# Index queries in packed chunks of 512, the index key beside two heads' queries, and three chunks in turn: one decoder layer on one core

## What is computed

```
h = rms_norm(x, norm_gain)                            # 256 x 2048
proj = einsum('bsd,dn->bsn', h, w_in)
qa, ka, va, ga   1024 columns each   # branch A: 8 heads x 128, sparse attention, its gate
qi 1024, ki 64, wi 16                # the index: 16 heads x 64, one shared key, 16 weights
qb, kb, vb, gb   1024 columns each   # branch B: differential attention, its gate
ma, mb           2048 columns each   # merge gates
qa, ka, qb, kb = rope(rms_norm(head, gain))           # per head of 128
qi, ki = rope(qi), rope(ki)                           # per head of 64, no norm
score = sum_h relu(qi_h . ki) * wi_h ; the top 64 keys of each query are kept in branch A
x + (sigmoid(ma) * (oa*silu(ga)) @ w_o_a + sigmoid(mb) * (ob*silu(gb)) @ w_o_b) @ w_out
```

## Time and profile before

| | us |
|---|---|
| median of 3 runs | 776.13 (774.92 to 776.16) |
| the profiled execution | 776.79 |
| its span | 775.0 |
| TensorE matmuls busy | 770.0 of 775.0 |
| VectorE busy | 510.5 |
| ScalarE busy | 423.6 |
| GpSimd busy | 132.8 |
| granted TensorE clock | 1.00 |

### The profile page before, as it was taken

How to read it: one execution, slowest core, us unless ns; L and a number is a source line. 1 busy time by engine, 2 the same in 40 slices (tenths; PEclk the granted TensorE clock), 3 DMA queues, 4 the chain that set the end, 5 groups by cost and what they waited for, 6 DMA issues and landing times.

```text
span 775.0 us, 10474 instructions
## 1 busy us (share of the span) xinstructions
PE 770.0 (99%) x3596; PEld 646.3 (83%) x3596; DVE 510.5 (66%) x718; ACT 423.6 (55%) x693; POOL 132.8 (17%) x225
## 2 busy tenths in 40 slices
PE   9999999999999999999999999999999999999998
PEld 8988888888888888888888888888888888888887
DVE  6679778778777655568656566566566567765553
ACT  7756665676654554555556554554676334444331
POOL 4405234322221000000222122203101011110000
PEclk9999999999999999999999999999999999999999
DMA  9897799988888675666767768867867888787553
GB/s 292 248 333 231 236 272 290 254 261 263 242 244 229 200 202 167 190 190 191 219 197 212 209 195 266 233 184 223 235 197 235 294 216 252 244 240 230 196 188 124
DMA packets 89579, 176.78 MB, mean 228 GB/s; under 512 B 7616, under 2 KB 15616, under 8 KB 89280
## 3 DMA queue, kind: packets, MB, share of 16 engines
q1 hardware_dynamic: 80752, 152.06, 65.0%
q0 software_dynamic: 8496, 23.87, 10.9%
q10 hardware_dynamic: 288, 0.30, 0.1%
HBM read 162.18 MB, written 14.02 MB: 227 GB/s over the span
## 4 chain that ended last, share of the span: by engine, by line
PE 93%; DMA 4%; DVE 1%; ACT 1%; SPq 1%; issue 0%
PE ps L718 30%; PE ps L719 30%; PE ps L720 29%; DMA raw<-in_w_in 4%; ACT hi L965 1%; DVE lo L1219 1%; PE ps L800 0%; PE ps L891 0%; PE ps L890 0%; PE ps L892 0%; SPq L444 0%; PE ps L788 0%; PE ps L801 0%; PE ps L802 0%; PE ps L803 0%
## 5 line engine op out<-in xcount | busy, mean ns | idle before, releaser
L1219 DVE TENSOR_TENSOR lo<-raw,hi 128x1024 fp32r<-128x1024 f32 (+2 forms) x279 | 333.8, 1202 | 237.7 <-ACT hi L965 236.7
L965 ACT ACTIVATE hi<-raw 128x1024 fp32r<-128x1024 f32 (+2 forms) x277 | 286.8, 1040 | 302.3 <-PE ps L720 265.7
L718 PE MATMUL ps<-hi,hT_hi 128*128 128x512 f32 (+1 forms) x912 | 353.0, 387 | 0.3 <-DVE lo L1219 0.3
L719 PE MATMUL ps<-lo,hT_hi 128*128 128x512 f32 (+1 forms) x912 | 352.6, 387 | 0.0
L720 PE MATMUL ps<-hi,hT_lo 128*128 128x512 f32 (+1 forms) x912 | 352.4, 386 | 0.0
L718 PEld LDWEIGHTS ps<-hi,hT_hi 128*128 128x128 f32 x912 | 171.2, 188 | 35.1 <-issue 0.5
L720 PEld LDWEIGHTS ps<-hi,hT_lo 128*128 128x128 f32 x912 | 171.2, 188 | 34.5
L719 PEld LDWEIGHTS ps<-lo,hT_hi 128*128 128x128 f32 x912 | 171.2, 188 | 33.5
L718 PE MATMUL ps<-hi,ogT_hi 128*128 128x512 f32 x128 | 49.8, 389 | 0.0
L719 PE MATMUL ps<-lo,ogT_hi 128*128 128x512 f32 x128 | 49.8, 389 | 0.0
L720 PE MATMUL ps<-hi,ogT_lo 128*128 128x512 f32 x128 | 49.8, 389 | 0.0
(11 more groups left out here) (182 smaller groups left out, 595.4 us busy)
## 6 DMA issues: line engine op xcount, KB each, us to landing
raw<-in_w_in SPq DMA_DIRECT2D x192, 512.0 KB, 4.4
raw<-in_w_out SPq DMA_DIRECT2D x32, 512.0 KB, 4.8
raw<-in_w_o_a SPq DMA_DIRECT2D x16, 512.0 KB, 6.5
raw<-in_w_o_b SPq DMA_DIRECT2D x16, 512.0 KB, 3.8
turned<-swapped POOLq DMA_DIRECT2D x12, 512.0 KB, 3.3
raw<-in_w_in SPq DMA_DIRECT2D x13, 384.0 KB, 4.9
v<-turned POOLq DMA_DIRECT2D x32, 128.0 KB, 6.0
raw<-in_w_in SPq DMA_DIRECT2D x8, 336.0 KB, 4.7
```

The source lines that it names most:

```text
L718: mm(o, a_hi, w_hi[:, j], start=first and j == 0, stop=False)
L719: mm(o, a_hi, w_lo[:, j], start=False, stop=False)
L965: activation(hi[:, slot, :, 0:width], raw[:, slot, :, 0:width], ACT.Copy).then_inc(hi_ready, 1)
L1219: tt(lo[:, slot, :, 0:width], raw[:, slot, :, 0:width], hi[:, slot, :, 0:width].bitcast(F32), ALU.subtract).then_inc(lo_ready, 1)
```

## The change

The columns of `w_in` are cut otherwise. The order of chunks and their places change with it:

| chunk | before | after |
|---|---|---|
| 0, 1 | qi, 384 columns, packed | qi, 512 columns, packed |
| 2 | 256 of qi, ki, wi: 336, ordinary | ki, wi and two heads of qb: 336, ordinary |
| 3, 4 | qa, 512 | three heads of qb each, 384 |
| 5, 6 | ka, 512 | kb, 512 |
| 7, 8 | qb, 512 | qa, 512 |
| 9, 10 | kb, 512 | ka, 512 |

The units of the first three chunks take turns: a unit of chunk 2 stands behind the pair i = 0, 1, 2, 4 and 6, and its last three stand at the end. Of the first three units the first k tile of each is computed before the second k tile of any. There are nine rounds, where there were eight (one for each of chunks 2 to 10); the first rounds are six places apart. The squares are written to `roped` and no longer to `swapped`, and wait for the transposition before. The index has two groups of four blocks and one that holds the key alone. Four transfers of x's rows and nine small rows are loaded at other places.

```diff
-X_OWN_AFTER = ((3, 0), (3, 2), (3, 4), (3, 6))
+SINES_AT = 12
+X_OWN_AFTER = ((3, 2), (3, 4), (3, 6), (4, 0))
+ROWS_AFTER = ((2, 5), (2, 6), (2, 7), (3, 0), (3, 1), (3, 3), (3, 5), (3, 7), (4, 1))
-IDX_W = (384, 384, 256 + KIWI)
-IDX_BLOCKS = tuple(w // P for w in IDX_W)
+FIRST_W = (512, 512, KIWI + 256, 384, 384)
+IDX_BLOCKS = (4, 4)
-C_QK, C_V, C_G, C_M = 3, 11, 15, 19
+C_QK, C_V, C_G, C_M = 2, 11, 15, 19
+QK_HEADS = ((0, 2), (0, 3), (1, 3)) + ((0, 4),) * 6
-FIRST_UNITS = tuple((c, i) for i in range(CK) for c in range(PACKED))
+THIRD_BEHIND = (0, 1, 2, 4, 6)
+FIRST_UNITS = tuple(unit for i in range(CK) for unit in
+                    ((0, i), (1, i)) + (((2, THIRD_BEHIND.index(i)),) if i in THIRD_BEHIND else ()))
+FIRST_UNITS += tuple((2, i) for i in range(len(THIRD_BEHIND), CK))
-INDEX_OUT = ((1, 7), (2, 4), (3, 3))
-INDEX_ROPE = (2 * CK, 3 * CK, 3 * CK + 4)
+INDEX_OUT = (2 * CK + 4, 3 * CK + 2)
+INDEX_ROPE = ((2 * CK + 5, 2 * CK + 6, 3 * CK, 3 * CK + 1), (3 * CK + 3, 3 * CK + 5, 3 * CK + 6, 3 * CK + 7))
+INDEX_KEY, INDEX_TAKEN, LAM_AT = 5 * CK + 6, 8 * CK + 3, 4 * CK + 4
-X_SQUARES = ((4, 0), (4, 1))
-LATER = {C_QK: 3, C_QK + 1: 2}
-LATE = {C_QK: 2, C_QK + 1: 1}
+X_SQUARES = ((4, 1), (4, 2))
+QK_OUT = (36, 42, 48, 54, 60, 66, 73, 80, 88)
+QK_COLUMNS = (46, 52, 58, 64, 70, 76, 83, 90, 96)
+QK_LOW = (48, 54, 60, 66, 72, 78, 85, 92, 96)
...
+            for j in range(2):
+                if j == 1:
+                    load_x(1)
+                for u in range(EARLY):
+                    load_first(u, j)
...
             def w_in_unit(c, i, bank, width=CW):
...
-                        pe.wait_ge(chunk_out, c - 1)
+                        pe.wait_ge(chunk_out, {4: 2, 5: 1, 6: 4}.get(c, c - 1) if isinstance(c, int) else c - 1)
...
+            for j in range(2):
+                for u in range(EARLY):
+                    rounded_part(u, j)
+                    low_part(u, j)
+            for u in range(EARLY, 3 * CK):
+                for j in range(2):
+                    rounded_part(u, j)
+                for j in range(2):
+                    low_part(u, j)
...
             def qk_chunk(n):
                 act.wait_ge(rope_done, n)
+                if isinstance(n, int) and n == PACKED:
+                    act.wait_ge(rstd_ready, 1)
...
-                    act.wait_ge(turned_kept, 16 * (n - C_QK))
+                if n == C_QK:
+                    act.wait_ge(ss_h_made, 1)
+                    act.wait_ge(index_turns, C_QK)
+                else:
+                    act.wait_ge(qk_turned, n - C_QK)
+                first, heads = QK_HEADS[n - C_QK]
                 for r in range(RT):
-                    for h in range(4):
+                    for h in range(first, first + heads):
...
-                        ins = activation(swapped[:, r, at], stage[:, r, at], ACT.Square,
+                        ins = activation(roped[:, r, at], stage[:, r, at], ACT.Square,
                                          accum_out=ss_h[:, j:j + 1])
```

More of the change, by code:

```diff
@@ L408, in build_layer @@
         index_turns, indexT_ready, index_lo_ready = sem("index_turns"), sem("indexT_ready"), sem("index_lo_ready")
-        index_kept, index_back = ([sem(f"index_{what}_{n}") for n in range(C_QK)] for what in ("kept", "back"))
+        index_kept, index_back = ([sem(f"index_{what}_{n}") for n in range(KEY_GROUP + 1)] for what in ("kept", "back"))
         idx_scores, idx_relu, idx_added = sem("idx_scores"), sem("idx_relu"), sem("idx_added")
@@ L457, in load_chunk, with load_small @@
                     load(i % RING, c * CK + i, w_in, 2 * i, col, width)
[L460 to L468, removed]
+            rows = [(gains[:, j], row) for j, row in enumerate((a_q_gain, a_k_gain, b_q_gain, b_k_gain))]
+            rows += [(lams[:, j], row) for j, row in enumerate((lambda_q1, lambda_k1, lambda_q2, lambda_k2))]
+            rows += [(sub_gain[:, :], b_subln_gain)]
+            def load_small(c, i):
+                if (c, i) in ROWS_AFTER:
+                    to, row = rows[ROWS_AFTER.index((c, i))]
+                    sp.dma_start(to, row[0].partition_broadcast(P)).then_inc(consts_landed, 16)
+                if (c, i) in X_OWN_AFTER:
+                    load_x_own(X_OWN_AFTER.index((c, i)))
+            for j in range(2):
[4 more added lines that the diff above has]
+            for u in range(EARLY, 3 * CK):
                 c, i = FIRST_UNITS[u]
@@ L471, in _ @@
                     load_x(i + 1)
-                load(u % RING, u, w_in, 2 * i, COL["qi"] + c * IDX_W[0], IDX_W[0])
+                load(u % RING, u, w_in, 2 * i, FIRST_COLS[c], FIRST_W[c])
                 if u == EARLY + 1:
                     sp.dma_start(pos_i[:, :], positions).then_inc(phases_landed, 16)
[L475 to L481, removed]
-                for i in range(CK):
[L483 to L493, removed]
+                load_small(c, i)
+            for c in range(3, len(FIRST_W)):
+                for i in range(CK):
+                    load(i % RING, c * CK + i, w_in, 2 * i, FIRST_COLS[c], FIRST_W[c])
+                    load_small(c, i)
+            with sp.Fori(0, 2) as n:
+                load_chunk(n + 5, n * CW + COL["kb"])
             with sp.Fori(0, 4) as n:
-                load_chunk(n + (C_QK + 4), n * CW + COL["qb"])
+                load_chunk(n + 7, n * CW)
             for c, name in ((C_V, "va"), (C_V + 2, "vb"), (C_G, "ga"), (C_G + 2, "gb")):
@@ L738, in early_unit @@
                         pe.wait_ge(x_again_first, 1)
                     mm(o_0, packed_rows(k), w_hi, start=first, stop=False)
-                for j in range(2):
-                    k, w_lo = 2 * unit_k + j, lo[:, u % RING, j, 0:IDX_W[0]]
-                    last = unit_k == CK - 1 and j == 1
-                    pe.wait_ge(lo_first if j == 0 and u == 0 else lo_ready, u + 1)
-                    mm(o_1, hT_hi[:, k, P:S], w_lo, start=False, stop=last)
-                    ins = mm(o_0, packed_rows(k), w_lo, start=False, stop=last)
@@ L1038, in _ @@
             x_hi_again(0).then_inc(x_again_first, 1)
+            for u in range(1, EARLY):
+                early_hi(u, 0)
             act.wait_ge(x_landed[1], 16)
```

386 lines of the change are left out of this document (209 added, 177 removed).

## The result

| | before | changed |
|---|---|---|
| median, runs of one chip session | 775.87 (774.92 to 776.16, 6 runs) | 781.15 (780.02 to 781.52, 6 runs) |
| ratio, 95% interval | | 1.0069 [1.0056, 1.0082] |
| profiled execution, span | 776.79, 775.0 | 781.2, 779.4 |
| start of chunk 11 | 224.96 | 229.37 |
| from there to the end of the span | 550.0 | 550.0 |

The changed kernel is 5.3 us slower. The forecast was 773.1 with a range of 770.9 to 775.6, so both the direction and the size were wrong. The last two lines of the table say where to look: all of the loss is ahead of chunk 11.

A forecast was written before the change was run, and what follows sets the result against it. TensorE's work plus its waits was taken as the bound. Terms of -1.7, -0.5, -1.2, +0.3 and +0.1 summed to -3.0 us, taking the median from 776.13 to 773.1, with an 8-in-10 range of 770.9 to 775.6.

The forecast's parts named there:

- TensorE's work: Up to chunk 11, 32 matmuls go from 512 to 384 columns: 1.7 us less.
- The start: First three units: first matmul 0.3 us later, waits 1.0 instead of 1.5 us: 0.5 us less (bounds 1.2 less, or nothing).
- The packed units: Packed units of 512 columns give loads more time: waits 0.2 instead of 1.4 us, 1.2 us less.
- Places 20 to 35: Index steps on narrow units, VectorE all but full: waits 1.0 instead of 0.7 us, 0.3 us more.
- DMA in the same stretch: Units 36 to 41 need 380 GB/s, six-unit periods with index returns 289 GB/s; nothing more counted in the sum.
- The rounds, six places apart: VectorE's work fits six units at 93%; each full round's root starts 0.6 us late: 0.1 us more (bounds 0 and 3).
- Rival 1's second half: The rounds' lateness adds up in full, 0.6 us in five rounds: 776.1 us; chance of the whole rival 0.13.
- the sign that was given: A TensorE gap over 3 us between units 24 and 70, with VectorE full, would show VectorE as the bound.
- Rival 2: DMA falls behind from place 34 to 60, 6.2 us on top: 779.3 us; chance 0.08.

The follow-up runs named there:

- Run 11: Changed kernel, one landing area, with GpSimd taking the roots of rounds 1 to 6 ahead of the return: 773.22 us, ratio 0.9974 to the kernel before.
- Run 1: Changed kernel with a second landing area, the returns alternating between the two: 775.42 us, ratio 1.0001 to the kernel before.
- 2: Changed kernel with the low parts of the first eight rounds one place earlier, one landing area: 777.05 us, ratio 1.0018 to the kernel before.
- 5: Changed kernel, one landing area, with GpSimd taking the next root ahead of the return in every round: 776.71 us, ratio 1.0014 to the kernel before.
- 6: Changed kernel with two landing areas and the root ahead of the return in every round: 776.88 us, ratio 1.0019 to the kernel before.
- run 7: Changed kernel, two landing areas, root always ahead of the return, columns and low part one place later where possible: 773.14 us, ratio 0.9971 to kernel before.
- 9: Changed kernel with two landing areas and the root ahead of the return for rounds 1 to 6 only: 773.35 us, ratio 0.9979 to kernel before.
- 10: Changed kernel, two landing areas, root first for rounds 1 to 6, returns of rounds 0 to 4 taken up one place later: 773.94 us, ratio 0.9978.

## Why the prediction was wrong, point by point

- **TensorE's work** (1.7 less): right, in counts and distances. Counts times distances are 216.7 before and 214.9 after.
- **The start** (0.5 less): right. The waits fell by 0.9 (1.5 to 0.6) and the first matmul comes 0.36 later: 0.6 less. The forecast named 0.3 for the later first matmul but did not add it to its sum, and took the waits as 1.0; the two misses nearly cancel.
- **The packed units** (1.2 less): right. 1.5 us of waits became 0.2: 1.3 less.
- **Places 20 to 35** (0.3 more, bounds 0.7 less and 5 more): inside its bounds. There were no waits, for 0.7 us before, so 0.7 less. VectorE was busy for 22.87 of the 27.7 us after chunk 3's start, and ScalarE was held for 2.35 us by `rstd`; the ring hid both. Two pairs of subtractions beside the tables took 2.39 and 2.23 us, where a pair took 1.82 ahead of them. The rule of the Trainium skill that the forecast weighed (GPSIMD Engine Reference, Specifications) is contention between VectorE and GpSimd at SBUF. These rows agree with it, and in this trace it put no wait on TensorE.
- **DMA in the same stretch** (nothing): right. Run 11 passes the rounds at 269 GB/s with no wait, and from 81.0 to 95.5, in units 36 to 41, the DMA engines moved 274 GB/s, not the 380 that the forecast had worked out. The Trainium skill (DMA: Bandwidth & Descriptors, Where 436 GB/s comes from) gives about 358 GB/s as a core's limit at HBM. These stretches stay below it, so they don't test it.
- **The rounds, six places apart**: this is the step that failed. "It holds ... The lateness stays under some 2 us, and the ring holds four units of 2.72. I take **0.1 us** (bounds 0 and 3)." Measured: 8.9 us. That VectorE's work fits into six places was right (65.0 of 78 us in run 11); the lateness of the root was not bounded. The text worked out GpSimd's list as 22.3 us against 21.7 and found each root "0.6 us late". Two things went wrong from there. First, it bounded the lateness, while it adds up: a late root makes VectorE's scaling late, which makes the transposition, the transfers and the next root late. What counts is the time round the loop against the period, and 0.6 us late in each of five rounds is 3.0. Run 1, which has only this loop, shows 3.5; its roots are 16.3 to 17.5 us apart, though, and not 16.9 each time. Second, it left out a link. It took the return's start from before, where the landing area had been free for 2 us, with the low part one subtraction behind the next round's transposition. With six places to a round it stands three places behind it. The return waits for it, and the loop grew from about 16.5 to between 17.4 and 18.3 us. That is the other 5.4 us.

The trace of the kernel before had one step of six places, from place 42 to 48: the root at 122.47 came 17.3 us after the one at 105.17, for a period of 16.3, and GpSimd had waited only 0.16 us for its squares. The next distance was eight, so the lateness ended there.

Run 11 checks the sum without the failed step: 773.2 for the 773.1 forecast. Part of that is luck. The kernel before measured 775.7 in that session, for the 776.1 that the forecast started from, so the gain is 2.0 to 2.5 us and not 3.0. In the traces it is 3.5, because the places 20 to 35 gave 1 us more than taken and other waits are left, 0.6 at the end of the front.

Rival 1's second half ("the rounds' lateness adds up in full") named the right place, and the sign that was given was there in sum, though not as one gap: between units 24 and 70 TensorE waited 6.7 us, at most 1.1 us of idle time at once, for VectorE's `lo`. But VectorE was not full there, and its price of 3 us lacked the loop through the low part. Rival 2 came nearest by its number, 779.3, with a mechanism that the runs refute. Both loops are shown by runs: the first by 1, 2 and 5, the second by 1 against 6. How the 3.5 us left in run 1 divide over its rounds is only read from its trace.

## What to carry to other kernels

When an engine's list holds a wait, ask what stands behind it, who waits for that, and whether that engine's list leads back to the wait. If so, add up the links once round and compare the sum with the period; below it lateness can die out, above it every round pays the difference, however idle both engines look. Pulling rounds together changes such sums twice, because the period shrinks and a step at a fixed distance moves past work of the next round. And the order of a list is right for a distance: the root ahead of the return took 7.1 us off at six places and cost 22 us at eight, where the columns were taken up too early for it; with a later take-up run 7 had it everywhere without that loss.

## What the hardware showed that I had not expected

The same GpSimd operation on 128x256 took either about 0.73 or about 1.45 us within one execution, in an order that changes from one to the next. Two rows of the changed kernel:

```profile
74.97 0.73 POOL L638 TENSOR_TENSOR g<-v 128x256 f32<-128x256 f32 x1
75.67 1.45 POOL L636 TENSOR_TENSOR g<-v 128x256 f32<-128x256 f32 x1
```

The nine table operations lasted 9.2 us in run 11 (73.77 to 82.93) and 10.6 in run 7, where they also began later (74.87 to 85.47). In run 7 ScalarE then waited longer for `rstd`, and TensorE was idle for 1.23 us at 91.40:

```profile
86.64 0.37 ACT L1051 ACTIVATE v<-ps 128x80 f32<-128x80 f32 x2 [3.85 <-POOL small L592]
```

The profiled executions of runs 7 and 9 both show this, with 1.5 us of waits in units 36 to 47, and both are 3 to 4 us above their medians; those of runs 10 and 11 don't and are not. Single executions of runs 7 and 9 to 11 reach 775 to 778, where most are at 772.3 to 774.5. The late tables may be a part of it, but those two traces also have 2.4 and 2.1 us of waits in units 48 to 75. What decides it was not tried.
